# A latent-trunk kernel: the fourth expert's transposed hidden rows in a buffer of their own, transposes two weight units up

## The chip, the core and the metric

The kernel runs on one core of one Trainium2 chip. The metric is the device time of one execution in microseconds (us). A core has five engines with queues of their own: TensorE (PE in the profile; its weight loads are PEld), VectorE (DVE), ScalarE (ACT), GpSimd (POOL) and SyncE (SP, which here issues the loads of the weights). They meet only at semaphores.

## What is computed

A two-layer trunk over 256 tokens of width 1024 (float32). Each layer has a mixer (attention and a short convolution in the first, a convolution module in the second) and then a mixture of experts: 16 experts in 4 groups of 4; a router picks for every token one group and two experts in it. Cut to what matters here:

```python
def moe_ffn(h, router_w, router_b, w1, w3, w2):
    t = h.reshape(-1, shape[-1])
    gates = route(t, router_w, router_b)
    out = jnp.zeros_like(t)
    for e in range(N_EXPERTS):
        y = (jax.nn.silu(t @ w1[e]) * (t @ w3[e])) @ w2[e]
        out = out + gates[:, e:e + 1] * y
```

w1[e] and w3[e] are 1024 x 512, w2[e] is 512 x 1024.

## The kernel before

**Precision.** Every product is made of three matmuls: an operand is rounded (`whi`, `xghi`, `hidThi`), the remainder is kept beside it (`wlo`, `xglo`, `hidTlo`), and `three` (L1822 to L1829) adds high by high, low by high and high by low. ScalarE does the roundings, VectorE the remainders.

**Turns and units.** A layer's experts run in four *turns*, one for a group of four experts and up to 128 gathered rows. In layer 0 all four turns are alike (three in a hardware loop, the fourth written out behind it, since it fetches no rows for a next turn). In layer 1 three are alike (two in the loop, the third behind it with `prepare`, in which the rows for a last turn are gathered with 32 matmuls, `gather`), and the last is the *wide* turn (`wide`), where each expert has its own rows. A turn runs through 48 *weight units* of 512 KB, j = 0 to 47, in the order of `expert_order`, four units for each matrix:

```
units  0-3 w1 e0    4-7 w3 e0    8-11 w1 e1   12-15 w3 e1  16-19 w2 e0  20-23 w1 e2
units 24-27 w3 e2  28-31 w2 e1  32-35 w1 e3   36-39 w3 e3  40-43 w2 e2  44-47 w2 e3
```

For every unit SyncE loads `raw` (8 slots, L550), ScalarE rounds it to `whi` (6 slots, `round_turn`, L796), VectorE subtracts to `wlo` (6 slots, `rest_turn`, L1463), and TensorE runs two times three matmuls of 512 columns (L1827 to L1829). ScalarE may round unit j once TensorE is through with unit j - 6 (it waits for `w_used` of j - 5 units); a `raw` slot is free for its next load when VectorE has subtracted the unit in it.

**Hidden rows.** After expert e's w1 and w3, ScalarE makes `silu` and VectorE `hid` (`hid_mul`, L1528, placed ahead of the subtraction of unit W13[e] + 13, which is 45 for the fourth expert). TensorE transposes `hid` in four pieces into bank BT of PSUM (`transpose_hidden`, L2205), ScalarE rounds it to `hidThi` (`hidT_round`, L966), VectorE makes `hidTlo` (`hidT_remainder`, L1533), and the expert's first w2 unit waits for that (`hidT_rest`). There is one pair `hidThi`, `hidTlo` for all experts.

**Where these steps stand** was set by one table, HID_T = [12, 20, 32, 44]: TensorE transposes ahead of unit HID_T[e]; ScalarE and VectorE do their step ahead of unit HID_T[e] + 6, and for the fourth expert, whose 50 lies beyond the turn, behind unit 47. In the looped turns TensorE also transposes the next turn's gathered rows (`xrow`, L2154, eight pieces, `rows_turned(0)`) right behind the fourth expert's hidden transposes, in the `prepare` turn it runs `gather` there (L2128), and both signal `gathered`. On that signal GpSimd fetches further rows, and ScalarE and VectorE round them (`xg_round`, L982 and L1491) after unit 1 of the next turn; ahead of the wide turn `xg_round` comes before the rounding of that turn's unit 0.

In the wide turn the previous turn's result is scattered at units 10, 13, 16 and 19 (`scatter`, L2198, which waits for VectorE's `x_add`, L1511), and the wide experts' own results are scattered from unit 46 on.

Of the kernel before, what the change touches and what calls it, by code (L numbers as in the profile page):

```python
# [12 lines left out]
P = 128  # L13
# [215 lines left out]
def program(nc, x, c, ctx, c_ctx, norm1_g, norm2_g, w_mod, b_mod, na_w_in, na_rpb, sc_conv_w, ab_w_out,  # L229
            cf_pw1_w, cf_pw1_b, cf_dw_w, cf_dw_b, cf_ln_g, cf_ln_b, cf_pw2_w, cf_pw2_b, router_w, router_b,  # L230
            moe_w1, moe_w3, moe_w2, final_g, consts, bias_scratch, mod_scratch, tok_scratch0, tok_scratch1, y_scratch0, y_scratch1, out):
    with ExitStack() as stack:
# [76 lines left out]
        hid = at("hid", [P, FF], 28)  # L309
        hidThi = at("hidThi", [P, FC, P], 30, F32R)  # L310
        hidTlo = at("hidTlo", [P, FC, P], 32, F32R)
        yg = at("yg", [P, D], 34)
        yhi = at("yhi", [P, D], 38, F32R)
        ylo = at("ylo", [P, D], 42, F32R)
# [175 lines left out]
        def mod_filled(eng, v):  # L490

            eng.wait_ge(mod_in[v % 4], 16 * ((v + 2) // 4))

        def moe_slot(tile, n):
            return tile[:, n % (RAW if tile is raw else SPL), :]
# [287 lines left out]
        def _(eng):  # L783
# [162 lines left out]
            def experts(L):  # L946
# [16 lines left out]

                def hidT_round(tn, e):
                    tn.wait(eng, "hid_T", e + 1)
                    A.copy(hidThi[:], ps[:, BT, :].rearrange("p (k n) -> p k n", k=4)).then_inc(tn.sem("hidT_rounded"), 1)  # L966

                def y_round(tn):
                    tn.wait(eng, "y_scaled", 1)
# [18 lines left out]
                def turn(tn, first=HEAD, ahead=HEAD):  # L988

                    for j in range(first, W_GROUP):  # L990
                        for e in range(PER_GROUP):
                            if j == W13[e] + 4 + 5:
                                silu_of(tn, e)
                            if j == HID_T[e] + 6:
                                hidT_round(tn, e)
                        round_turn(tn, j)
                    hidT_round(tn, PER_GROUP - 1)
                    for j in range(W_GROUP, W_GROUP + ahead):
                        round_turn(tn, j)
                    if ahead:  # L1000
                        xg_round(tn.g, 1)
# [17 lines left out]
                def wide(i):  # L1019
                    tn = wide_turn(i)  # L1020
                    if i:
                        gate_copy(tn)
                        wide_xg_round(tn, i, 0)
                    for j in range(W_GROUP):
                        for a in range(2):
                            if j == WIDE_SPREAD[a] + 7:
                                spread_copy(tn, a)
                        if j == 8 and i == 0:
                            y_round(Turn(L, GROUPS - 1, sems))
                        for e in range(PER_GROUP):  # L1030
                            if j == W13[e] + 4 + 5:
                                silu_of(tn, e)
                            if j == HID_T[e] + 6:
                                hidT_round(tn, e)
                            if e and j == WIDE_GATHER[e] + 4 + e // 2 * 2:
                                wide_xg_round(tn, i, e)
                            if j == WIDE_Y[e] + 8:
                                wide_y_round(tn, e)
                        round_turn(tn, j)
                    hidT_round(tn, PER_GROUP - 1)  # L1040
                    for e in range(2, PER_GROUP):
                        wide_y_round(tn, e)

# [101 lines left out]
        def _(eng):  # L1145
# [207 lines left out]
            def experts(L):  # L1353
# [176 lines left out]

                def hidT_remainder(tn, e):
                    tn.wait(eng, "hidT_rounded", e + 1)
                    V.tensor_tensor(hidTlo[:], ps[:, BT, :].rearrange("p (k n) -> p k n", k=4), hidThi[:], ALU.subtract) \  # L1533
                     .then_inc(tn.sem("hidT_rest"), 1)

                def wide_select():
# [23 lines left out]
                def turn(tn, first=HEAD, ahead=HEAD, prepare=False):  # L1560

                    looped = tn.spill is None
                    for j in range(first, W_GROUP):
                        if prepare and j == 10:
                            wide_select()
                        if prepare and j == WIDE_PREFIX + 8:
                            wide_places()
                        if looped:
                            if j == 5:
                                y_scale(tn)  # L1570
                        for e in range(PER_GROUP):
                            if j == W13[e] + 8 + 5:
                                hid_mul(tn, e)
                            if j == HID_T[e] + 6:
                                hidT_remainder(tn, e)
                        if looped and not ahead and j == BACK:
                            at_ = tn.g + C_SLOT
                            link(set_spread(cst[:, at_:at_ + 1]))
                            eng.wait_ge(y_back, 16 * (L + 1))
                            for t in range(NT):  # L1580
                                link(V.tensor_tensor(xres[:, t, :], xres[:, t, :], yback[:, t, :], ALU.add))
                        rest_turn(tn, j)
                    hidT_remainder(tn, PER_GROUP - 1)
                    for j in range(W_GROUP, W_GROUP + ahead):
                        rest_turn(tn, j)
                    if ahead:
                        xg_remainder(tn.g, 1)
# [31 lines left out]
                def wide(i):  # L1619
# [12 lines left out]
                    for j in range(W_GROUP):  # L1632
# [7 lines left out]
                        for e in range(PER_GROUP):  # L1640
                            if j == W13[e] + 8 + 5:
                                if e == 0:
                                    tn.wait(eng, "spread_set", 1)
                                hid_mul(tn, e)
                            if j == HID_T[e] + 6:
                                hidT_remainder(tn, e)
                            if e and j == WIDE_GATHER[e] + 4 + e // 2 * 2:
                                wide_xg_rest(tn, i, e)
                            if j == WIDE_Y[e] + 5:
                                wide_y_scale(tn, e)  # L1650
                            if j == WIDE_Y[e] + 9:
                                wide_y_rest(tn, e)
# [2 lines left out]
                                if j == SCATTER[k] + 6:  # L1655
                                    x_add(last, k)
                        rest_turn(tn, j)
                    hidT_remainder(tn, PER_GROUP - 1)
                    for e in range(2, PER_GROUP):
                        wide_y_scale(tn, e)  # L1660
                        wide_y_rest(tn, e)
# [159 lines left out]
        def _(eng):  # L1821
# [275 lines left out]
            def experts(L):  # L2097
# [112 lines left out]
                def turn(tn, prepare=False, ahead=True):  # L2210
                    looped = tn.spill is None
                    for j in range(W_GROUP):
# [19 lines left out]
                        if name == "w2":  # L2232
                            if q == 0:
                                tn.wait(eng, "hidT_rest", e + 1)
                            for half in range(2):
                                cut = slice(half * HALF, (half + 1) * HALF)
                                ins = three(ps[:, BY + half, :], hidThi[:, q, :], hidTlo[:, q, :],
                                            moe_slot(whi, n)[:, cut], moe_slot(wlo, n)[:, cut],
                                            e == 0 and q == 0, e == PER_GROUP - 1 and q == 3)
                        else:  # L2240
# [36 lines left out]
                def wide(i):  # L2277
# [8 lines left out]
                    for j in range(W_GROUP):  # L2286
# [27 lines left out]
                        if name == "w2":  # L2314
# [3 lines left out]
                                    tn.wait(eng, "y_scaled", min(e, 2))  # L2318
                            for half in range(2):
                                cut = slice(half * HALF, (half + 1) * HALF)  # L2320
                                ins = three(ps[:, WIDE_BY[e] + half, :], hidThi[:, q, :], hidTlo[:, q, :],
                                            moe_slot(whi, n)[:, cut], moe_slot(wlo, n)[:, cut], q == 0, q == 3)
                        else:
                            if name == "w1" and q == 0 and (e or i):
# [137 lines left out]

W13 = [expert_order().index((e, "w1")) * 4 for e in range(PER_GROUP)]

HID_T = [12, 20, 32, 44]
SCATTER = [10, 13, 16, 19]

XG_AT = 2
# [96 lines left out]
```

## Time and profile before

| | us |
|---|---|
| median of 3 runs (lowest, highest) | 1009.28 (1009.09, 1009.70) |
| the profiled execution | 1009.37 |
| its span, first to last instruction | 1007.6 |

So 1.8 us of the profiled execution lie around its span, and it stands 0.09 us over the median. The mean granted TensorE clock over the span is 0.986 of full speed.

A row of the timeline is: start in us from the span's start, duration, engine, line, operation, output<-inputs, shapes, count; in brackets the idle time of that engine ahead of it, and what ended it. Matmuls are pipelined and their ends are modelled: the next one starts before the end that is written, so a stream is best read from start to start. "issue" is idle time for which the profile shows no releaser.

### The profile page before, as it was taken

The page shows a single profiled execution, that of the slowest core. Times are in us where ns is not written, and L with a number is a line of the kernel's source. Part 1 is how long each engine was busy: PE and PEld are TensorE (multiplying, and loading weights), DVE is VectorE, ACT ScalarE, POOL GpSimd, SP SyncE. Part 2 cuts the span into 40 slices and gives each one's busy share as a digit, 9 for nine tenths or more (in the row PEclk, how much of TensorE's full clock was granted, in tenths as well). Part 3 has the DMA queues.
Part 4 walks back from the last instruction along what each step waited for, and adds up shares of the span by engine and source line. Part 5 has one row for each costly group of instructions (what it writes and reads, how often), then busy time and mean ns, then how long its engine had stood idle before and what let it go on. Part 6 is the DMA issues. An engine that isn't in the chain of part 4 may idle for free.

```text
span 1007.6 us, 16757 instructions
## 1 busy us (share of the span) xinstructions
PE 954.8 (95%) x6004; PEld 758.9 (75%) x6004; DVE 754.3 (75%) x929; ACT 620.5 (62%) x769; POOL 113.6 (11%) x181
## 2 busy tenths in 40 slices
PE   5899999999999999999978999898999999999995
PEld 3688885788887878878857885677787878888784
DVE  1544378558998989989966634666998989888994
ACT  3824326435878778777844424426888877758772
POOL 3290000103001000000000632010001000000000
PEclk9999999999999999999998999999999999999999
DMA  9997859669999999999969765929999999988971
GB/s 364 354 259 260 285 197 336 208 259 298 395 396 360 392 370 359 395 338 382 392 229 307 206 214 160 368 83 369 396 396 360 393 376 344 392 330 277 353 272 44
DMA packets 145810, 314.07 MB, mean 312 GB/s; under 512 B 12904, under 2 KB 43920, under 8 KB 145736
## 3 DMA queue, kind: packets, MB, share of 16 engines
q1 hardware_dynamic: 135360, 286.53, 79.5%
q0 software_dynamic: 10048, 26.45, 7.8%
q8 instruction: 45, 0.74, 0.3%
q14 instruction: 29, 0.24, 0.1%
q10 hardware_dynamic: 328, 0.11, 0.0%
HBM read 298.64 MB, written 9.75 MB: 306 GB/s over the span
## 4 chain that ended last, share of the span: by engine, by line
PE 79%; DVE 8%; DMA 7%; issue 2%; ACT 2%; SPq 0%; DVEq 0%; ACTq 0%
PE ps L1827 17%; PE ps L1829 16%; PE ps L1828 16%; DMA raw<-in_w_mod 3%; PE ps L2390 3%; DMA raw<-in_moe_w 3%; PE ps L1839 2%; DVE wlo L1463 2%; PE ps L1929 2%; PE ps L1931 2%; PE ps L1930 2%; PE ps L2416 2%; PE ps L2417 2%; PE ps L2418 2%; PE ps L1947 1%
## 5 line engine op out<-in xcount | busy, mean ns | idle before, releaser
L1463 DVE TENSOR_TENSOR wlo<-raw,whi 128x1024 fp32r<-128x1024 f32 x384 | 454.4, 1220 | 40.7 <-ACT whi L796 37.6
L796 ACT CAST whi<-raw 128x1024 fp32r<-128x1024 f32 x384 | 398.5, 1052 | 109.9 <-PE ps L1829 75.3
L1827 PE MATMUL ps<-whi,xghi 128*128 128x512 f32 x480 | 193.7, 404 | 3.7 <-DVE wlo L1463 2.6
L1829 PE MATMUL ps<-wlo,xghi 128*128 128x512 f32 x480 | 190.6, 397 | 0.0
L1828 PE MATMUL ps<-whi,xglo 128*128 128x512 f32 x480 | 190.6, 397 | 0.0
L1827 PEld LDWEIGHTS ps<-whi,xghi 128*128 128x128 f32 x480 | 91.0, 190 | 26.8 <-DVE wlo L1463 6.0
L1827 PE MATMUL ps<-whi,hidThi 128*128 128x512 f32 x256 | 102.6, 401 | 6.6 <-DVE hidTlo L1533 5.2
L1829 PEld LDWEIGHTS ps<-wlo,xghi 128*128 128x128 f32 x480 | 91.1, 190 | 21.6
L1828 PEld LDWEIGHTS ps<-whi,xglo 128*128 128x128 f32 x480 | 91.3, 190 | 20.2
L1158 DVE TENSOR_TENSOR wlo<-raw,whi 128x1024 fp32r<-128x1024 f32 x56 | 73.0, 1338 | 40.5 <-ACT whi L791 40.3
L1829 PE MATMUL ps<-wlo,hidThi 128*128 128x512 f32 x256 | 101.8, 398 | 0.0
L1828 PE MATMUL ps<-whi,hidTlo 128*128 128x512 f32 x256 | 101.6, 397 | 0.0
L791 ACT CAST whi<-raw 128x1024 fp32r<-128x1024 f32 x56 | 56.8, 1046 | 44.3 <-DMA raw<-in_na_w_in 18.5
L1839 PE MATMUL ps<-raw,pair 128*32 128x256 f32 x768 | 58.7, 413 | 10.6 <-DMA raw<-in_w_mod 7.6
L1827 PEld LDWEIGHTS ps<-whi,hidThi 128*128 128x128 f32 x256 | 48.6, 190 | 19.5 <-issue 7.5
L1829 PEld LDWEIGHTS ps<-wlo,hidThi 128*128 128x128 f32 x256 | 48.5, 189 | 11.5
L1828 PEld LDWEIGHTS ps<-whi,hidTlo 128*128 128x128 f32 x256 | 48.6, 190 | 11.1
L1839 PEld LDWEIGHTS ps<-raw,pair 128*32 128x32 f32 x768 | 20.5, 115 | 32.6 <-issue 14.9
L1929 PE MATMUL ps<-hThi,whi 128*128 128x256 f32 (+1 forms) x144 | 44.2, 307 | 0.1
L1931 PE MATMUL ps<-hTlo,whi 128*128 128x256 f32 (+1 forms) x144 | 42.3, 294 | 0.0
L1930 PE MATMUL ps<-hThi,wlo 128*128 128x256 f32 (+1 forms) x144 | 42.3, 294 | 0.0
L2416 PE MATMUL ps<-fThi,whi 128*128 128x256 f32 x128 | 37.3, 292 | 3.2 <-DVE fTlo L1748 3.2
(354 smaller groups left out, 1455.6 us busy)
## 6 DMA issues: line engine op xcount, KB each, us to landing
raw<-in_moe_w SPq DMA_DIRECT2D x384, 512.0 KB, 6.7
raw<-in_w_mod SPq DMA_DIRECT2D x96, 512.0 KB, 6.9
raw<-in_na_w_in SPq DMA_DIRECT2D x24, 512.0 KB, 8.9
raw<-in_cf_pw_w SPq DMA_DIRECT2D x24, 512.0 KB, 8.6
mods<-mod_scratch POOLq DMA_DIRECT2D x9, 512.0 KB, 6.5
raw<-in_ab_w_out SPq DMA_DIRECT2D x8, 512.0 KB, 5.9
urep<-uT SPq DMA_DIRECT2D x64, 35.5 KB, 2.9
urep<-uT POOLq DMA_DIRECT2D x64, 35.5 KB, 2.5
```

The lines of the kernel that those rows point to most:

```text
L791: A.copy(whi[:, n % SPL, :], raw[:, u % RAW, :]).then_inc(w_rounded, 1)
L796: A.copy(whi[:, (MOE_W[tn.L] + j) % SPL, :], raw[:, (MOE_U[tn.L] + j) % RAW, :]).then_inc(tn.sem("w_rounded"), 1)
L1158: V.tensor_tensor(wlo[:, n % SPL, :], raw[:, u % RAW, :], whi[:, n % SPL, :], ALU.subtract).then_inc(unit_done, 1)
L1463: V.tensor_tensor(wlo[:, n % SPL, :], raw[:, (MOE_U[L] + j) % RAW, :], whi[:, n % SPL, :], ALU.subtract).then_inc(tn.sem("unit_done"), 1)
L1827: T.matmul(dst, lhi, rhi, start=first, stop=False)
L1828: T.matmul(dst, llo, rhi, start=False, stop=False)
L1829: return T.matmul(dst, lhi, rlo, start=False, stop=last)
L1839: ins = T.matmul(ps[q * QUAD:(q + 1) * QUAD, bank, 0:QW], pair[:, k, :], raw[:, u % RAW, q * QW:(q + 1) * QW], start=(k == 0), stop=(k == ...
L1929: T.matmul(dst, wpart(n0, k, 0, m * P, P), acts(k, 0), start=(k == 0), stop=False)
L1930: i2 = T.matmul(dst, wpart(n0, k, 1, m * P, P), acts(k, 0), start=False, stop=False)
L1931: i3 = T.matmul(dst, wpart(n0, k, 0, m * P, P), acts(k, 1), start=False, stop=(k == KC - 1))
L2416: T.matmul(dst, wpart2(done_n, k, 0, m * P, P), a0, start=(k == 0), stop=False)
```

## The change

- HID_T[3] goes from 44 to 42, so the fourth expert's transposes, and with them the rows' transposes or the `gather`, stand ahead of unit 42, in the middle of the third expert's w2.
- A table HID_ROUND = [18, 26, 38, 47] takes the place of HID_T[e] + 6. For the first three experts the values are the same. The fourth expert's rounding and remainder stand ahead of unit 47 now, not behind it.
- Since units 42 and 43 still read the third expert's `hidThi` and `hidTlo`, the fourth expert gets its own pair: `lastThi`, `lastTlo` in looped turns, `wideThi`, `wideTlo` in the wide turn. `hidden_T` picks the pair.

```diff
+        last_hidT = (at("lastThi", [P, FC, P], 46, F32R), at("lastTlo", [P, FC, P], 48, F32R))
+        wide_hidT = (at("wideThi", [P, FC, P], 68, F32R), at("wideTlo", [P, FC, P], 70, F32R))
...
+        def hidden_T(tn, e):
+
+            return (hidThi, hidTlo) if e < PER_GROUP - 1 else wide_hidT if tn.after else last_hidT
...
-                    A.copy(hidThi[:], ps[:, BT, :].rearrange("p (k n) -> p k n", k=4)).then_inc(tn.sem("hidT_rounded"), 1)
+                    A.copy(hidden_T(tn, e)[0][:], ps[:, BT, :].rearrange("p (k n) -> p k n", k=4)).then_inc(tn.sem("hidT_rounded"), 1)
...
-                            if j == HID_T[e] + 6:
+                            if j == HID_ROUND[e]:
                                 hidT_round(tn, e)
                         round_turn(tn, j)
-                    hidT_round(tn, PER_GROUP - 1)
...
-                            if j == HID_T[e] + 6:
+                            if j == HID_ROUND[e]:
                                 hidT_remainder(tn, e)
...
-                    hidT_remainder(tn, PER_GROUP - 1)
...
-                                ins = three(ps[:, BY + half, :], hidThi[:, q, :], hidTlo[:, q, :],
+                                ins = three(ps[:, BY + half, :], hidden_T(tn, e)[0][:, q, :], hidden_T(tn, e)[1][:, q, :],
...
-HID_T = [12, 20, 32, 44]
+HID_T = [12, 20, 32, 42]
+HID_ROUND = [18, 26, 38, 47]
```

**TensorE, looped turn of layer 0**, before: the last matmuls of unit 43, the transposes of `hid` and of the rows, and unit 44.

```order
L1828 MATMUL ps<-whi,hidTlo 128x512
L1829 MATMUL ps<-wlo,hidThi 128x512
L207 REGISTER_ALU
L2205 MATMUL ps<-cst,hid 128x128 [waits hid_set]
L2205 MATMUL ps<-cst,hid 128x128 x3
L2229 ISA
L2154 MATMUL ps<-cst,xrow 128x128 [waits rows_of]
L2154 MATMUL ps<-cst,xrow 128x128 x7
L207 REGISTER_ALU
L1827 MATMUL ps<-whi,hidThi 128x512 [waits hidT_rest,unit_done]
```

The same in the changed kernel (its lines are three higher); what follows is unit 42.

```order
L1831 MATMUL ps<-whi,hidTlo 128x512
L1832 MATMUL ps<-wlo,hidThi 128x512
L207 REGISTER_ALU
L2208 MATMUL ps<-cst,hid 128x128 [waits hid_set]
L2208 MATMUL ps<-cst,hid 128x128 x3
L2232 ISA
L2157 MATMUL ps<-cst,xrow 128x128 [waits rows_of]
L2157 MATMUL ps<-cst,xrow 128x128 x7
L207 REGISTER_ALU
L1830 MATMUL ps<-whi,hidThi 128x512 [waits unit_done]
```

Unit 44, two units on, carries the wait for `hidT_rest` and reads `lastThi`. **VectorE, layer 0's last turn**, before:

```order
L1528 SCALAR_TENSOR_TENSOR hid<-silu,gturn,ps 128x512 [waits w_used,silu_set]
L1463 TENSOR_TENSOR wlo<-raw,whi 128x1024 [waits w_rounded] x3
L1533 TENSOR_TENSOR hidTlo<-ps,hidThi 128x512 [waits hidT_rounded]
L1483 TENSOR_TENSOR yg<-ps,g2keep 128x512 [waits y_put,w_used]
L1483 TENSOR_TENSOR yg<-ps,g2keep 128x512
```

and in the changed kernel:

```order
L1532 SCALAR_TENSOR_TENSOR hid<-silu,gturn,ps 128x512 [waits w_used,silu_set]
L1467 TENSOR_TENSOR wlo<-raw,whi 128x1024 [waits w_rounded] x2
L1538 TENSOR_TENSOR lastTlo<-ps,lastThi 128x512 [waits hidT_rounded]
L1467 TENSOR_TENSOR wlo<-raw,whi 128x1024 [waits w_rounded]
L1487 TENSOR_TENSOR yg<-ps,g2keep 128x512 [waits y_put,w_used]
```

The remainder of the fourth expert's hidden rows moved ahead of the subtraction of unit 47; `hid` itself stays where it was, ahead of unit 45's. **ScalarE, end of the wide turn**, before:

```order
L796 CAST whi<-raw 128x1024 [waits w_used,raw_in5]
L796 CAST whi<-raw 128x1024 [waits w_used,raw_in6]
L796 CAST whi<-raw 128x1024 [waits w_used,raw_in7]
L966 CAST hidThi<-ps 128x512 [waits hid_T]
L1012 CAST yhi_107<-yg 128x1024 [waits y_scaled]
```

and in the changed kernel:

```order
L802 CAST whi<-raw 128x1024 [waits w_used,raw_in5]
L802 CAST whi<-raw 128x1024 [waits w_used,raw_in6]
L972 CAST wideThi<-ps 128x512 [waits hid_T]
L802 CAST whi<-raw 128x1024 [waits w_used,raw_in7]
L1017 CAST yhi_111<-yg 128x1024 [waits y_scaled]
```

The rounding of the hidden rows moved ahead of that of unit 47; no engine's count of these instructions changed.

## Rows read from the trace of the kernel before

**Rows 1.** Page, sections 1 and 4: busy by engine, chain by engine
```profile
PE 954.8 (95%) x6004; PEld 758.9 (75%) x6004; DVE 754.3 (75%) x929; ACT 620.5 (62%) x769; POOL 113.6 (11%) x181
...
PE 79%; DVE 8%; DMA 7%; issue 2%; ACT 2%; SPq 0%; DVEq 0%; ACTq 0%
```

**Rows 2.** Tile view, who waited for hidTlo: us in total, times
```profile
  PE ps L1827: 5.2, 7
```

**Rows 3.** Timeline (start, duration in us), end of layer 0's first turn
```profile
299.38 0.40 PE L1827 MATMUL ps<-whi,hidThi 128*128 128x512 f32 x1
...
302.19 0.60 PE L2205 MATMUL ps<-cst,hid 128*128 128x128 f32 x4
...
302.62 1.04 PE L2154 MATMUL ps<-cst,xrow 128*128 128x128 f32 x8
...
302.82 0.59 ACT L966 CAST hidThi<-ps 128x512 fp32r<-128x512 f32 x1 [2.19 <-PE ps L2205]
...
303.44 0.69 DVE L1533 TENSOR_TENSOR hidTlo<-ps,hidThi 128x512 fp32r<-128x512 f32 x1 [1.55 <-ACT hidThi L966]
...
304.28 0.47 PE L1827 MATMUL ps<-whi,hidThi 128*128 128x512 f32 x1 [0.62 <-DVE hidTlo L1533]
```

**Rows 4.** Timeline, four transposes whose result nobody waits for
```profile
256.12 0.60 PE L2205 MATMUL ps<-cst,hid 128*128 128x128 f32 x4
...
256.48 0.48 PE L1827 MATMUL ps<-whi,xghi 128*128 128x512 f32 x1
```

**Rows 5.** Timeline, TensorE, end of layer 0's last turn
```profile
513.73 0.60 PE L2205 MATMUL ps<-cst,hid 128*128 128x128 f32 x4
...
515.82 0.47 PE L1827 MATMUL ps<-whi,hidThi 128*128 128x512 f32 x1 [1.49 <-DVE hidTlo L1533]
```

**Rows 6.** Timeline, TensorE, end of the wide turn
```profile
983.02 0.60 PE L2205 MATMUL ps<-cst,hid 128*128 128x128 f32 x4
...
985.06 0.47 PE L1827 MATMUL ps<-whi,hidThi 128*128 128x512 f32 x1 [1.45 <-issue]
```

**Rows 7.** Timeline, TensorE, end of layer 1's last looped turn
```profile
904.36 3.74 PE L2128 MATMUL ps<-pick,htok 128*128 128x128 f32 x32
...
907.86 0.48 PE L1827 MATMUL ps<-whi,hidThi 128*128 128x512 f32 x1
```

**Rows 8.** Timeline, start of the wide turn, three engines
```profile
908.14 1.07 ACT L982 CAST xghi<-ps 128x512 fp32r<-128x512 f32 x2 [2.99 <-PE ps L2128]
...
910.20 2.36 DVE L1463 TENSOR_TENSOR wlo<-raw,whi 128x1024 fp32r<-128x1024 f32 x2 [3.99 <-ACT whi L796]
...
913.81 0.50 PE L1827 MATMUL ps<-whi,xghi 128*128 128x512 f32 x1
...
920.60 1.08 ACT L1006 CAST xg2hi<-ps 128x512 fp32r<-128x512 f32 x2 [1.21 <-PE ps L2154]
...
940.22 0.50 PE L2198 MATMUL ps<-yhi,spread 128*128 128x512 f32 x1 [0.68 <-DVE xres L1511]
```

**Rows 9.** Timeline, VectorE and ScalarE beside units 40 to 43, three turns
```profile
297.60 0.74 DVE L1528 SCALAR_TENSOR_TENSOR hid<-silu,gturn,ps 128x512 f32<-128x512 f32 x1
...
298.26 3.63 DVE L1463 TENSOR_TENSOR wlo<-raw,whi 128x1024 fp32r<-128x1024 f32 x3
...
299.58 1.05 ACT L796 CAST whi<-raw 128x1024 fp32r<-128x1024 f32 x1 [0.35 <-PE ps L1829]
...
509.93 0.74 DVE L1528 SCALAR_TENSOR_TENSOR hid<-silu,gturn,ps 128x512 f32<-128x512 f32 x1
...
979.05 0.73 DVE L1528 SCALAR_TENSOR_TENSOR hid<-silu,gate_of,ps 128x512 f32<-128x512 f32 x1
```

**Rows 10.** SyncE's waits (us, times, longest); issues: KB, us to landing
```profile
SPq L550 <- DVE wlo L1463: 377.9, 368, 14.5
...
raw<-in_moe_w SPq DMA_DIRECT2D x384, 512.0 KB, 6.7
```

**Rows 11.** One stretch: busy PE, PEld, DVE, ACT, POOL; PEclk, DMA, GB/s
```profile
896.70:900.30 3.60, 3.60 (x11) 2.82 (x11) 2.63 (x3) 0.94 (x1) 0.00 (x0) 0.56 1.01 377
```

More of the change, by code:

```diff
@@ L1039, in wide @@
                         round_turn(tn, j)
-                    hidT_round(tn, PER_GROUP - 1)
                     for e in range(2, PER_GROUP):
@@ L1532, in hidT_remainder @@
                     tn.wait(eng, "hidT_rounded", e + 1)
-                    V.tensor_tensor(hidTlo[:], ps[:, BT, :].rearrange("p (k n) -> p k n", k=4), hidThi[:], ALU.subtract) \
+                    hi, lo = hidden_T(tn, e)
+                    V.tensor_tensor(lo[:], ps[:, BT, :].rearrange("p (k n) -> p k n", k=4), hi[:], ALU.subtract) \
                      .then_inc(tn.sem("hidT_rest"), 1)
@@ L1573, in turn @@
                                 hid_mul(tn, e)
-                            if j == HID_T[e] + 6:
+                            if j == HID_ROUND[e]:
                                 hidT_remainder(tn, e)
@@ L1644, in wide @@
                                 hid_mul(tn, e)
-                            if j == HID_T[e] + 6:
+                            if j == HID_ROUND[e]:
                                 hidT_remainder(tn, e)
@@ L1657, in wide @@
                         rest_turn(tn, j)
-                    hidT_remainder(tn, PER_GROUP - 1)
                     for e in range(2, PER_GROUP):
@@ L2320, in wide @@
                                 cut = slice(half * HALF, (half + 1) * HALF)
-                                ins = three(ps[:, WIDE_BY[e] + half, :], hidThi[:, q, :], hidTlo[:, q, :],
+                                ins = three(ps[:, WIDE_BY[e] + half, :], hidden_T(tn, e)[0][:, q, :], hidden_T(tn, e)[1][:, q, :],
                                             moe_slot(whi, n)[:, cut], moe_slot(wlo, n)[:, cut], q == 0, q == 3)
```

## The prediction

> **What bounds the kernel now.** I read the page first. TensorE is busy for 95% of the span and holds 79% of the chain that ended last; VectorE and the DMA hold 8% and 7% [rows 1]. "Busy" alone proves little here, since the ends of matmuls are modelled, so I went to the timeline of a looped turn and read from start to start. Unit 42 starts at 299.38 and the transposes behind unit 43 at 302.19 [rows 3]: 12 matmuls in 2.81 us, 0.234 us each, 1.40 us a unit. 288 such matmuls are 67.4 us; the turns of layer 0 follow each other in 70.5 us (the hidden transposes stand at 302.19 in the first turn and at 513.73 in the fourth, three turns on [rows 3, 5]). So in a turn TensorE streams, and only what interrupts the stream counts. The next view is who waits for the tile `hidTlo`: TensorE, 7 times, 5.2 us [rows 2]. The timeline shows the place: behind unit 43 the transposes run, then ScalarE rounds, VectorE subtracts, and only then does unit 44 start [rows 3]. Nothing else of that turn's end is exposed.
>
> **The stall, by turn.** What the stall costs is not the idle time in the brackets, since it is counted from modelled ends, but the distance of the starts less what the transposes cost when nobody waits for them. Four of those take 0.36 us from their start to the next unit's [rows 4]; the gather's 32 matmuls, of the same shape, go in 3.50 us, 0.11 each [rows 7], so eight rows' transposes are 0.87.
> - Looped turn with rows' transposes: 304.28 - 302.19 - 0.36 - 0.87 = 0.86 us [rows 3]. There are five: turns 1 to 3 of layer 0 and 1 and 2 of layer 1, all with the same 0.62 us in the bracket (5 x 0.62 + 1.49 for the next case leave 0.6 of the 5.2 us for the seventh wait, the first expert's in layer 1's first turn, which the change doesn't touch). 5 x 0.86 = 4.3 us.
> - Last turn of layer 0, without rows: 515.82 - 513.73 - 0.36 = 1.73 us [rows 5].
> - Wide turn: 985.06 - 983.02 - 0.36 = 1.68 us [rows 6]. The view calls it "issue", but the order of the work is the same.
> - `prepare` turn: none, the gather covers it; unit 44 starts right behind it [rows 7].
>
> The sum is 7.7 us. By the brackets alone it would be 5 x 0.62 + 1.49 + 1.45 = 6.0 us [rows 3, 5, 6]; I take the distances and keep 6.0 as the low end.
>
> **Does the change remove it all?** The transposes move, they don't multiply: four of `hid`, eight of the rows or the gather, at the same cost, ahead of unit 42. What has to be ready there is `hid`. In the steady turn VectorE finishes it at 298.34, unit 42 starts at 299.38 [rows 3, 9]: 1.0 us to spare. In layer 0's last turn `hid` is finished at 510.67 and unit 42 stands two units ahead of 513.73, at 510.92: 0.25 us. In the wide turn it is 979.78 against 980.21: 0.43 us [rows 5, 6, 9]. From VectorE's end to TensorE's start 0.15 us pass (303.44 + 0.69 to 304.28 [rows 3]), so both just hold, with 0.10 us left in the tighter one.
>
> Then the new pair has to be ready at unit 44. ScalarE starts its rounding 0.63 us after the transposes start and takes 0.59 [rows 3]. VectorE has the subtractions of units 45 and 46 ahead of the remainder, 1.21 us each (3.63 for three [rows 9]). Steady turn: VectorE is free at 298.26 + 2.42 = 300.68, ScalarE is ready at 299.38 + 0.63 + 0.59 = 300.60, the remainder is there at about 301.4, unit 44 would start at 299.38 + 1.23 + 2.81 = 303.42. Last turn of layer 0: 510.67 + 2.42 + 0.69 + 0.15 = 513.9 against 510.92 + 0.36 + 2.81 = 514.1. Wide turn: 979.78 + 3.26 = 983.0 against 983.4. So nothing of the stall should be left, though the last two are covered by 0.2 and 0.4 us only. If that cover is gone, the excess comes back us for us.
>
> What stands behind the moved steps in the queues: on ScalarE the rounding of unit 47, which would have started at 299.58 [rows 9], waits for the transposes and the new rounding and ends near 301.7; VectorE's subtraction of unit 47 ends near 302.9, where before it ended at 301.89 (298.26 + 3.63). Unit 47 itself is due on TensorE at 303.42 + 3 x 1.40 = 307.6. The SyncE load into that slot is issued 1.0 us later; it lands 6.7 us after issue [rows 10], at 309.6, and TensorE is through with unit 1 of the next turn, on which its rounding (unit 7's) waits anyway, near 303.42 + 6 x 1.40 = 311.8. That hides it. The first roundings of the next turn had been held up behind the old rounding and are no longer. The move to other buffers costs nothing: same shapes, same engines.
>
> **The start of the wide turn.** The moved gather has a second effect. Before, ScalarE waits 2.99 us for it and VectorE then stands idle for 3.99 us, until 910.20 [rows 8], and from there VectorE is late twice: the wide turn's first unit starts at 913.81, where 907.86 + 4 x 1.40 + 0.08 = 913.54 would do (0.27 us), and the scatter at 940.22 shows 0.68 us in the bracket, which is 0.85 from start to start, since a modelled end lies 0.17 behind the pace. With the gather two units up it ends at 905.05; ScalarE can round unit 0 when unit 42 is through, at 906.45, and VectorE starts at about 907.6, 2.6 us earlier. Not all of it lasts. At 920.60 ScalarE waits 1.21 us for TensorE's own transposes of the second expert's rows [rows 8], and they come at most 0.27 us earlier; there VectorE's lead shrinks to some 0.6 us. I take 0.55 us for the whole, with 0.27 as the low end (the first wait alone) and 1.12 as the high one (both).
>
> **Sum.** 7.7 + 0.55 = 8.25 us off the profiled execution's 1009.37: 1001.1; off the median, 0.09 lower, 1001.0. From the low ends (6.0 + 0.27) to the high ones (7.7 + 1.12) it is 1003.0 to 1000.5. Layer 0's share should come through to the end: in the code the loads of the second mixer's first matrices wait for slots that TensorE itself frees behind the last turn.
>
> **Rivals.**
> 1. *The thin covers don't hold.* In layer 0's last turn and in the wide turn either `hid` comes late to unit 42 or the remainder late to unit 44. For it: 0.10 to 0.4 us of slack. Against it: the sums above are made of measured durations. If half of 1.73 + 1.68 stays, the time is 1001.0 + 1.7 = 1002.7; if all of it stays, 1004.4.
> 2. *The clock.* Between 896.7 and 900.3 the granted clock is 0.56 [rows 11], half speed in the main (1.2 of 2.4 GHz), behind a run of one-column products in the `prepare` turn. It costs (1 - 0.56) x 3.6 = 1.6 us. The change shifts everything behind it by some us, so such a stretch may grow, shrink or fall away: 1001.0 plus or minus 1.6. Against it: the stretch begins 4 us ahead of the place that changes in that turn. The Trainium skill (TensorE: Matmul & The Clock Gate, "What's actually happening") says that the window by which the clock is set runs on its own and does not start with the kernel. By that rule, one such stretch appearing or vanishing would give 1002.6 or 999.4; the trace shows the stretches but not what sets where they end.
> 3. *The loads become the bound (slower).* The place is the slot of unit 47, refilled 1.0 us later in each of the eight turns while TensorE wants its successor 0.9 us earlier. By the sum above the load lands 2.2 us before it is needed. From a landing later by more than that, each further us is paid in every turn. From 1.0 us over it the gain is gone (8 x 1.0 against 8.25); at 1.3 us over it the time is 1009.3 + 10.4 - 8.25 = 1011.5. For it: SyncE waits 368 times for VectorE's subtractions [rows 10], so a late subtraction does hold up loads. Against it: the 2.2 us, and that the first roundings of each next turn are freed.
> 4. *The stall only changes its place:* unit 42 waits as long for `hid` as unit 44 did for the remainder. Within 0.2% of before. Only `hid` 2 us later than in [rows 9] would do that.
>
> **How the numbers follow.** Forecast 0.68, thin covers 0.12, clock 0.14 (half to each side), loads 0.03, stall in a new place 0.03. The range takes the bounds of the sum, most of the thin covers and either clock case: 999.4 to 1003.8. A measurement of this kernel can tell about 0.2%, 2 us, from no change. Faster by over that: the first three, 0.94; within it 0.03; slower 0.03.
>
> **What would show it.** TensorE's waits for the tiles `lastTlo` and `wideTlo` absent from the views (the one wait for `hidTlo` left is the first expert's in layer 1's first turn); transposes of `hid` two units behind unit 41's end with 0.36 us to the next start; the period of layer 0's turns 0.9 us shorter, 69.6; VectorE starting the wide turn's unit 0 some 2.6 us earlier against TensorE, and no more than half of the wait at the scatter left. The forecast is wrong if TensorE's rows show idle time ahead of the transposes (rival 1 or 4), if ScalarE's roundings of units 5 to 8 of a turn wait for the DMA (rival 3), or if stretches with a clock under 1 lie elsewhere or last longer (rival 2).

## The result, and the profile after

| | before | changed |
|---|---|---|
| median (lowest, highest) | 1009.49 (1009.09, 1010.46), 4 runs | 1001.10 (999.59, 1002.17), 4 runs |
| the profiled execution | 1009.37 | 999.59 |
| its span | 1007.6 | 997.8 |
| mean granted clock | 0.986 | 0.985 |

The ratio of the changed kernel to the one before is 0.9896, with a 95% interval of 0.9868 to 0.9923. It is faster by more than the 0.2% that the prediction named. The median lies at the forecast, 1001.0; but the ratio, taken on 1009.28, gives 998.8 (996.0 to 1001.5), just under the range of the prediction, which ended at 999.4, and the profiled execution lost 9.8 us where 8.25 were forecast. The ratio is not the quotient of the two medians: that is 0.9917, 8.4 us. Why the two differ, the eight times do not show.

The page of the changed kernel, the same two lines as in [rows 1]:

```profile
PE 954.2 (96%) x6004; PEld 757.9 (76%) x6004; DVE 751.0 (75%) x929; ACT 620.7 (62%) x769; POOL 114.8 (12%) x181
...
PE 79%; DMA 9%; DVE 7%; ACT 2%; issue 2%; SPq 1%; DVEq 0%; ACTq 0%
```

The shares hardly move, since the stall was never more than 1% of the span. The view of the tile `lastTlo` says what became of it. Its lines are the instructions that write it, the idle time ahead of them, and who waited for it:

```profile
L1538 DVE TENSOR_TENSOR lastTlo<-ps,lastThi x7: 683/692/692, 302.7 to 895.0; 128x512 fp32r<-128x512 f32 x7
its engine sat idle before it (us, times) until:
who waited for it (us, times):
```

There is nothing under "who waited", and nothing under the idle times. Before, TensorE waited 7 times for the remainder [rows 2]; the one wait of the changed kernel, 0.2 us for `hidTlo`, is the first expert's in layer 1's first turn. The end of a looped turn, to be read against [rows 3] (timeline of TensorE; start, duration):

```profile
301.41 0.60 PE L2208 MATMUL ps<-cst,hid 128*128 128x128 f32 x4
...
301.84 1.04 PE L2157 MATMUL ps<-cst,xrow 128*128 128x128 f32 x8
...
302.64 0.47 PE L1830 MATMUL ps<-whi,hidThi 128*128 128x512 f32 x1
```

This is unit 42's start now, not unit 44's: 302.64 - 301.41 = 1.23 us for all twelve transposes, the 0.36 + 0.87 of the prediction. In layer 0's last turn (against [rows 5]), VectorE's `hid`, TensorE's transposes and unit 42, VectorE's remainder, and the step from unit 43 to unit 44:

```profile
509.83 0.74 DVE L1532 SCALAR_TENSOR_TENSOR hid<-silu,gturn,ps 128x512 f32<-128x512 f32 x1
...
510.82 0.60 PE L2208 MATMUL ps<-cst,hid 128*128 128x128 f32 x4
...
511.18 0.48 PE L1830 MATMUL ps<-whi,hidThi 128*128 128x512 f32 x1
...
512.76 0.68 DVE L1538 TENSOR_TENSOR lastTlo<-ps,lastThi 128x512 fp32r<-128x512 f32 x1
...
513.83 0.40 PE L1832 MATMUL ps<-wlo,hidThi 128*128 128x512 f32 x1
...
514.06 0.39 PE L1830 MATMUL ps<-whi,lastThi 128*128 128x512 f32 x1
```

`hid` ends at 510.57, the transposes start at 510.82; the remainder ends at 513.44, unit 44 starts at 514.06 and only 0.23 us behind its predecessor: no wait. The two margins are 0.25 and 0.6 us. In the wide turn (against [rows 6]) it is the same, 0.23 us from unit 43 to unit 44:

```profile
975.26 0.39 PE L1832 MATMUL ps<-wlo,hidThi 128*128 128x512 f32 x1
...
975.49 0.40 PE L1830 MATMUL ps<-whi,wideThi 128*128 128x512 f32 x1
```

The start of the wide turn, to be read against [rows 7, 8]:

```profile
894.19 3.74 PE L2131 MATMUL ps<-pick,htok 128*128 128x128 f32 x32
...
897.68 0.48 PE L1830 MATMUL ps<-whi,hidThi 128*128 128x512 f32 x1
...
897.96 1.07 ACT L988 CAST xghi<-ps 128x512 fp32r<-128x512 f32 x2 [2.04 <-PE ps L2131]
...
900.49 1.23 DVE L1467 TENSOR_TENSOR wlo<-raw,whi 128x1024 fp32r<-128x1024 f32 x1 [2.98 <-ACT whi L802]
...
906.13 0.39 PE L1830 MATMUL ps<-whi,xghi 128*128 128x512 f32 x1
...
912.77 0.59 ACT L1011 CAST xg2hi<-ps 128x512 fp32r<-128x512 f32 x1 [1.59 <-PE ps L2157]
...
932.24 0.50 PE L2201 MATMUL ps<-yhi,spread 128*128 128x512 f32 x1 [0.52 <-DVE xres L1515]
```

The gather ends two units earlier; ScalarE rounds its result at 897.96 at once, VectorE stands idle for 2.98 us in place of 3.99 and begins the wide turn's subtractions at 900.49, 5.6 us ahead of TensorE's first unit of that turn (906.13). Before, it was 3.6 us ahead (913.81 - 910.20), so the lead grew by 2.0 us where the prediction had 2.6. At 912.77 ScalarE waits 1.59 us for the second expert's rows, and the wait at the scatter is 0.52 us in place of 0.68.

**Where the 9.8 us are.** The spans, cut at the same instructions in five profiles (two of the kernel before, three of the changed one; e1, e2 and e12 are runs of the study below). All times are from start to start.

| stretch | before | e2, before | changed | e1, changed | e12, changed |
|---|---|---|---|---|---|
| start to layer 0's first unit | 237.76 | 237.75 | 238.70 | 241.85 | 237.55 |
| to its first hidden transposes | 18.36 | 18.38 | 19.44 | 18.99 | 18.36 |
| **to the scatter of its last turn** | 267.68 | 267.79 | 263.82 | 263.84 | 264.15 |
| second mixer, to layer 1's first unit | 164.38 | 166.08 | 162.55 | 167.07 | 163.45 |
| to its first hidden transposes | 22.11 | 20.66 | 21.99 | 22.07 | 22.47 |
| **two turns on** | 141.81 | 141.87 | 139.77 | 139.72 | 139.51 |
| **to the wide turn's first hidden transposes** | 79.93 | 79.89 | 77.93 | 79.47 | 79.49 |
| **to the last scatter** | 66.36 | 66.40 | 64.53 | 64.56 | 64.48 |
| to the end | 9.21 | 9.08 | 9.07 | 9.03 | 9.04 |

The bold rows hold what the change touches. They lose 9.7 us between the two first profiles, but 8.2 to 8.4 us between the two profiles of the kernel before and e1 or e12. The difference is in the main one thing, a stretch at half speed in the `prepare` turn. The other rows differ by up to 4.5 us among profiles in which their code is the same, and in the first two the time goes with the granted clock: from the start to layer 0's first unit it is 1.00 where the stretch takes 237.6 to 237.8 us, 0.99 at 238.7 and 0.97 at 241.9; from there to the first hidden transposes 0.91 at 18.4, 0.88 at 19.0 and 0.85 at 19.4. In the second mixer it runs from 0.93 to 0.97, the two shortest times at 0.97 and 0.95, the longest at 0.94.

### The profile page after: what moved, and what is told of

It is laid out like the page before. It is cut to its first block, busy times and chain, and to the rows that moved or that the text cites. A ratio compares the mean times of both kernels' runs of the same rounds, so it can differ in the third digit from the quotient of the medians.

```text
span 997.8 us, 16757 instructions
## 1 busy us (share of the span) xinstructions
PE 954.2 (96%) x6004; PEld 757.9 (76%) x6004; DVE 751.0 (75%) x929; ACT 620.7 (62%) x769; POOL 114.8 (12%) x181
## 4 chain that ended last, share of the span: by engine, by line
PE 79%; DMA 9%; DVE 7%; ACT 2%; issue 2%; SPq 1%; DVEq 0%; ACTq 0%
PE ps L1830 17%; PE ps L1832 17%; PE ps L1831 17%; DMA raw<-in_w_mod 3%; DMA raw<-in_na_w_in 3%; PE ps L2393 3%; PE ps L1842 2%; DMA raw<-in_moe_w 2%; PE ps L2419 2%; DVE wlo L1467 2%; PE ps L2420 2%; PE ps L2421 2%; PE ps L1932 1%; PE ps L2208 1%; PE ps L1933 1%
## 5 line engine op out<-in xcount | busy, mean ns | idle before, releaser
L1830 PE MATMUL ps<-whi,hidThi 128*128 128x512 f32 x192 | 76.8, 400 | 0.2 <-DVE hidTlo L1538 0.2
L1832 PE MATMUL ps<-wlo,hidThi 128*128 128x512 f32 x192 | 75.9, 395 | 0.0
L1831 PE MATMUL ps<-whi,hidTlo 128*128 128x512 f32 x192 | 75.7, 395 | 0.0
L1830 PEld LDWEIGHTS ps<-whi,hidThi 128*128 128x128 f32 x192 | 36.1, 188 | 8.7 <-issue 0.6
L1832 PEld LDWEIGHTS ps<-wlo,hidThi 128*128 128x128 f32 x192 | 36.1, 188 | 8.6
L1831 PEld LDWEIGHTS ps<-whi,hidTlo 128*128 128x128 f32 x192 | 36.1, 188 | 8.1
L711 POOL DMA_INDIRECT xrow<-tok_scratch,places x8 | 8.8, 1103 | 268.7 <-PE ps L2157 204.9
```

The lines of the kernel that those rows point to most:

```text
L1830: T.matmul(dst, lhi, rhi, start=first, stop=False)
L1831: T.matmul(dst, llo, rhi, start=False, stop=False)
L1832: return T.matmul(dst, lhi, rlo, start=False, stop=last)
```

## Experiments

Runs of one chip stand side by side: e1 to e4, e5 to e8, and e9 to e12. The kernel before had a median of 1013.43 (23 runs, 1007.62 to 1017.63), 1012.50 (19 runs, 1008.06 to 1016.83) and 1011.64 (11 runs, 1007.76 to 1015.69) there.

**e1, e2: both kernels once more, unaltered.**

> The changed kernel once more, unaltered, for its spread and its clock. Theory A (the change takes away TensorE's stall at the fourth expert's w2, 7.1 to 7.7 us, and 0.4 us at the start of the wide turn; what the first profile showed beyond that, 1.6 us of half-speed clock missing in the prepare turn and 1.8 us less in the second mixer, is chance): median 1001 to 1002, and in this profile a half-speed stretch may well stand in the prepare turn again. Theory B (the change itself also removes the half-speed stretch and shortens the second mixer): 999.5 in most runs, no stretch in the prepare turn, second mixer again 162.5 us from the first scatter to the first unit of layer 1.

> The kernel before, unaltered, for a second profile. Both theories: 1009 to 1010.5. Theory A: the half-speed stretches stand at other places or have other lengths than in the first profile. Theory B: the stretch of 3.6 us in the prepare turn is there again, and the second mixer again takes 164.4 us.

Measured: e1 1005.59 (6 runs, 999.65 to 1008.40), ratio 0.9914 (0.9885 to 0.9944); e2 1011.93 (10 runs, 1006.97 to 1017.97), ratio to the same code 0.9993 (0.9966 to 1.0021). The absolute medians miss the expectations, e1's by 3.6 us and e2's by 1.4 us; this chip's runs of the kernel before spread over 10 us, where the first four lay within 1.4. The ratio of e1, taken on 1009.28, gives 1000.6, inside the prediction's range. What the two theories say of the changed kernel came out for A. The busy times, clock, DMA share and GB/s of two stretches, the second mixer and the 3.6 us behind the one-column products of the `prepare` turn; first the changed kernel's first profile, then e1:

```profile
521.96:684.51 162.55, 151.32 (x1543) 116.77 (x1543) 91.50 (x154) 62.01 (x97) 39.29 (x77) 0.97 0.70 224
...
890.90:894.50 3.60, 3.60 (x21) 3.03 (x21) 3.41 (x4) 1.17 (x2) 0.00 (x0) 1.00 1.03 383
```

```profile
524.68:691.75 167.07, 153.87 (x1543) 118.88 (x1543) 91.62 (x154) 61.97 (x97) 39.15 (x77) 0.94 0.68 217
...
898.10:901.70 3.60, 3.60 (x11) 2.85 (x11) 2.67 (x3) 0.79 (x1) 0.00 (x0) 0.54 1.04 360
```

The last but two number is the granted clock. The stretch that was missing (1.00) is back in e1 (0.54), and the second mixer took 167.07 us at a clock of 0.94 in place of 162.55 at 0.97. The kernel before had 0.56 [rows 11] and, in its second mixer:

```profile
523.80:688.18 164.38, 151.46 (x1543) 117.94 (x1543) 91.75 (x154) 61.99 (x97) 39.18 (x77) 0.96 0.68 220
```

So these 1.6 and 1.8 us of the first profile are not of the change. Theory B falls. In e2 the half-speed stretch stood behind the one-column products again, with eight matmuls at half pace for seven (granted clock 0.60 from 897.1 to 900.7), which speaks for neither; but the second mixer took 166.08 us there, not the 164.4 of theory B.

**e3: the hidden transposes alone.** Edit on the changed kernel:

```diff
                             if j == HID_T[ee]:
                                 transpose_hidden(tn, ee)
-                                if looped and ee == PER_GROUP - 1 and ahead:
-                                    if prepare:
-                                        gather(tn.g + 1)
-                                    else:
-                                        eng.wait_ge(rows_of, ...)
-                                        rows_turned(0).then_inc(gathered, 1)
+                        if looped and ahead:
+                            if prepare and j == 44:
+                                gather(tn.g + 1)
+                            if not prepare and j == 44:
+                                eng.wait_ge(rows_of, ...)
+                                rows_turned(0).then_inc(gathered, 1)
```

> Only the fourth expert's hidden transposes move up to unit 42; the rows' transposes and the gather stay ahead of unit 44. Theory A: the stall is gone all the same, since the hidden rows are ready 0.9 us or more before unit 44; only the early start of VectorE in the wide turn is lost, 0.4 us: 1001.5. Rival (the gain comes with the rows and the gather): 1005 or more. VectorE would stand idle for about 4 us ahead of the wide turn again.

Measured: 1003.70 (6 runs), ratio 0.9911 (0.9886 to 0.9936), as e1's; the time is 2.2 us over the expected one, on the chip on which e1's was over it too. The periods of layer 0's turns are 69.53, 69.72 and 69.68 us, 0.1 us under the changed kernel's 69.80. The gather's share is seen at the wide turn, VectorE's start and TensorE's scatter:

```profile
905.77 2.36 DVE L1467 TENSOR_TENSOR wlo<-raw,whi 128x1024 fp32r<-128x1024 f32 x2 [5.28 <-ACT whi L802]
...
935.79 0.50 PE L2201 MATMUL ps<-yhi,spread 128*128 128x512 f32 x1 [0.68 <-DVE xres L1515]
```

VectorE is idle for 5.28 us, more than the 3.99 before the change, and the wait at the scatter is 0.68 us, as before the change; the turn from `prepare` to wide takes 79.86 us where e1 takes 79.47. So the stall goes with the hidden rows alone, and the gather is worth 0.4 us.

**e4: the transposes up, but one pair of buffers.** The fourth expert's rounding waits until unit 43 is through and stands behind unit 47's, the remainder too:

```diff
-            return (hidThi, hidTlo) if e < PER_GROUP - 1 else wide_hidT if tn.after else last_hidT
+            return (hidThi, hidTlo)
...
                     tn.wait(eng, "hid_T", e + 1)
+                    if e == PER_GROUP - 1:
+                        tn.wait(eng, "w_used", 44)
...
-HID_ROUND = [18, 26, 38, 47]
+HID_ROUND = [18, 26, 38, 99]
```

> Transposes two units up as in the change, but the fourth expert uses the common pair hidThi and hidTlo, so that ScalarE must wait until unit 43 is through, and rounds behind unit 47's rounding, as before. Theory A: each of the eight turns then waits at unit 44 for ScalarE (0.15 + 0.59), VectorE (0.03 + 0.69) and 0.15 back, with nothing as cover: 1.6 to 1.8 us each, 13 to 14 us over the changed kernel, 1014 to 1015, slower than before. Rival (the position of the transposes alone brings the gain and the buffer is incidental): 1001 to 1003.

Measured: 1016.48 (10 runs), ratio to the kernel before 1.0045 (1.0023 to 1.0068): slower, and by the ratios 13.2 us over e1. The end of layer 0's first turn, ScalarE, VectorE, TensorE:

```profile
308.24 0.59 ACT L974 CAST hidThi<-ps 128x512 fp32r<-128x512 f32 x1 [3.04 <-PE ps L1838]
...
308.85 0.69 DVE L1542 TENSOR_TENSOR hidTlo<-ps,hidThi 128x512 fp32r<-128x512 f32 x1 [2.40 <-ACT hidThi L974]
...
309.69 0.47 PE L1836 MATMUL ps<-whi,hidThi 128*128 128x512 f32 x1 [1.49 <-DVE hidTlo L1542]
```

1.49 us of idle time here; from start to start unit 44 comes 1.66 us later than the pace of 0.23 us, and so it is in every one of the eight turns (1.65 to 1.72), 13.3 us in all. Without the second pair the move does harm.

**e5, e6: one unit lower and one unit higher** (HID_T = [12, 20, 32, 43] and [12, 20, 32, 41]).

> The changed kernel with the fourth expert's transposes, rows and gather ahead of unit 43 instead of 42. From the start of the transposes it takes 0.63 + 0.59 + 0.03 + 0.69 + 0.15 = 2.1 us until the remainder is usable. A looped turn with rows gives 0.36 + 0.87 + 1.40 = 2.6 us of cover: no stall. Layer 0's last turn and the wide turn give 0.36 + 1.40 = 1.8 us: 0.3 us of stall each. Theory A: 0.6 to 0.8 us over the changed kernel. Rival (VectorE's queue, not the cover, sets it: it has unit 46's subtraction ahead): no more than 0.1 us of stall in the two.

> The changed kernel with the transposes ahead of unit 41. Theory A: now hid is late. It is finished 0.36 us (steady turn), 1.15 us (layer 0's last turn) and 0.97 us (wide turn) after unit 40 is through, plus 0.15 us to TensorE: stalls of 0.5 us in five turns, 1.3 and 1.1 us in the two, none in the prepare turn, 4.9 us in all, ahead of the transposes: 1006 beside a changed kernel of 1001. Rival (what VectorE has done by then moves up with TensorE, so hid comes in time): under 1 us.

Measured: e5 1006.47 (6 runs), ratio 0.9930 (0.9901 to 0.9959). In layer 0's last turn, the transposes and the last matmul of unit 43, VectorE's remainder, and unit 44:

```profile
516.01 0.60 PE L2208 MATMUL ps<-cst,hid 128*128 128x128 f32 x4
...
517.60 0.40 PE L1832 MATMUL ps<-wlo,hidThi 128*128 128x512 f32 x1
...
517.26 0.69 DVE L1538 TENSOR_TENSOR lastTlo<-ps,lastThi 128x512 fp32r<-128x512 f32 x1 [0.29 <-ACT lastThi L972]
...
518.10 0.47 PE L1830 MATMUL ps<-whi,lastThi 128*128 128x512 f32 x1
```

From 517.60 to 518.10 are 0.50 us, 0.27 over the pace, and in the wide turn 0.22 over it; no looped turn waits. That is theory A's 0.3 us (0.5 in the two turns together, too little for the times to tell), and VectorE waits for ScalarE there (0.29 us), not TensorE for VectorE's other work. e6 measured 1009.68 (10 runs), ratio 0.9965 (0.9944 to 0.9985). Its transposes in the first and the last turn of layer 0 and in the wide turn:

```profile
302.62 0.65 PE L2208 MATMUL ps<-cst,hid 128*128 128x128 f32 x4 [0.25 <-DVE hid L1532]
...
513.80 0.66 PE L2208 MATMUL ps<-cst,hid 128*128 128x128 f32 x4 [1.04 <-DVE hid L1532]
...
980.87 0.66 PE L2208 MATMUL ps<-cst,hid 128*128 128x128 f32 x4 [0.83 <-DVE hid L1532]
```

Now the idle time stands ahead of the transposes and the releaser is `hid`. From start to start it is 0.42 to 0.45 us in five turns, 1.20 and 0.99 us in the two others, 4.3 us in all against the 4.9 expected, and 5.1 us over e1 by the ratios. So of the three places 42 is the right one: at 41 `hid` is late, at 43 the remainder.

**e7: rows back at 44, gather at 42** (the edit of e3 with `prepare and j == 42`).

> The changed kernel with the rows' transposes of the looped turns back ahead of unit 44, but the gather of the prepare turn ahead of unit 42. Theory A: both gains together: periods of layer 0's turns 69.5 to 69.8 us, the wait at the scatter in the wide turn 0.69 us as in the changed kernel against 0.85 with the gather at unit 44. Time equal to the changed kernel's within 0.5 us. Rival (the gather's place is of no use): wait at the scatter 0.85 us and the prepare turn 0.4 us longer.

Measured: 1004.96 (6 runs), ratio 0.9919 (0.9890 to 0.9947). The periods are 69.67, 69.68, 69.68 us, the wait at the scatter 0.68 us from start to start, as e1's (0.85 before). As expected, within what the times can tell.

**e8 to e11: the one-column products cut in two.** In the `prepare` turn 28 one-column products stand ahead of unit 40. Edit:

```diff
-                        if prepare and j == WIDE_PREFIX + 12:
-                            wide_gates(0)
+                        if prepare and j in (WIDE_PREFIX + 12, WIDE_PREFIX + 13):
+                            wide_gates(0, (j - WIDE_PREFIX - 12,))
```

where part 0 runs the 16 for the gates and part 1 the 12 for the row numbers, with the signal. e8 and e11 are this on the changed kernel; e9 and e10 have e7's edit too.

> The changed kernel with the 28 one-column products of the prepare turn (3.0 us in one run ahead of unit 40) cut in two: 16 ahead of unit 40, 12 ahead of unit 41. Theory A with the clock as a rule of its own: the stretch of 2.6 to 3.6 us at half speed behind them, which stood in four of six profiles and costs about 1.6 us, does not appear; the prepare turn to wide turn period is 77.9 us as in the one profile of the changed kernel without a stretch. Rival (the stretch has to do with the time of the chip, not with these products): it stands there at half speed as often as before, period 79.5 us.

> The changed kernel with the two alterations joined: rows' transposes back ahead of unit 44 (gather stays at 42), and the one-column products cut in two. Expected from the traces: 5 x 0.12 us from the rows, about 1.2 us on average from the half-speed stretch that no longer stands in the prepare turn: 1.8 us under the changed kernel on the same chip. Rival (the stretch's absence in e8 was chance, as it was in two of nine profiles with the products in one run): the stretch is there in most of the next three profiles, and the gain is 0.6 us.

> The same kernel for one more profile. Products cut in two prevent the half-speed stretch: none in the prepare turn, from the first expert's transposes there to those of the wide turn 77.8 us. Rival: stretch of about 3 us, 79.4 us.

> The kernel of e8 for one more profile. Same expectation: no half-speed stretch in the prepare turn, 77.9 us. Rival: 79.5 us.

> The changed kernel for a third profile, beside the three with the products cut in two. By both theories the stretch stands here in about seven of ten cases (79.5 us), and the five looped turns and the fourth expert's step show no stall.

(The "four of six" of e8's expectation was a miscount: it was five of six.) The two parts in e8, and the 3.6 us behind the first:

```profile
892.70 1.84 PE L2175 MATMUL ps<-wsel,pick 128*128 128x1 f32 x16
...
895.88 1.39 PE L2182 MATMUL ps<-cst,pick 128*128 128x1 f32 x12
...
894.40:898.00 3.60, 3.60 (x24) 3.21 (x24) 3.60 (x4) 1.04 (x1) 0.00 (x0) 1.00 1.02 374
```

The granted clock stays at 1.00, and so it does over 892 to 899, behind both parts. With the products in one run, a stretch of 6 to 8 matmuls at half the pace followed in 8 of 10 profiles (not in the changed kernel's first and in e6); cut in two, in none of 4. From the `prepare` turn's first hidden transposes to the wide turn's the four take 77.92, 77.90, 77.91 and 77.93 us, and e12, in one run again, 79.49. By time: e8 1004.22, ratio 0.9910 (0.9880 to 0.9940); e9 1000.98 (6 runs), ratio 0.9892 (0.9862 to 0.9922); e10, e11 and e12, single executions, 1000.74, 1005.98 and 1000.39. e9 is the fastest kernel of the study by its ratio, but its interval overlaps those of e1 and e7 and the changed kernel's first (0.9896), and the one execution of the changed kernel on its chip, e12, was as fast: the 1.8 us expected for e9 cannot be read from the times. That it is better than the changed kernel rests on the trace, by 0.12 us in each of five turns and 1.6 us in the `prepare` turn.

e12 also misses its expectation in one place. In layer 0's last turn of this execution of the changed kernel TensorE does wait for `hid`. VectorE's `hid`, the end of unit 41 and the transposes:

```profile
508.08 0.74 DVE L1532 SCALAR_TENSOR_TENSOR hid<-silu,gturn,ps 128x512 f32<-128x512 f32 x1
...
508.40 0.40 PE L1832 MATMUL ps<-wlo,hidThi 128*128 128x512 f32 x1
...
508.87 0.66 PE L2208 MATMUL ps<-cst,hid 128*128 128x128 f32 x4
```

`hid` ends at 508.82, 0.05 us ahead of the transposes, and from 508.40 to 508.87 are 0.24 us over the pace. In the other eight profiles of this placement (hidden transposes at unit 42, a pair of their own) there is no such wait, though in e3 `hid` ends only 0.06 us ahead of the transposes, in the others 0.24 to 0.26. In the 60 us up to these transposes ScalarE waited for loads 21 times in e12, 7.6 us in all, and 7 to 11 times in the others, 2.4 to 3.9 us; that this is why VectorE came late is likely, but not shown.

## Why the prediction was right or wrong

**Right, and shown:** what bounds the kernel, the place of the stall, that it goes altogether (no wait for `lastTlo` or `wideTlo`), and that the gather helps the wide turn. The thin covers hold in the main. In layer 0's last turn `hid` has 0.25 us to spare, as worked out, and the remainder 0.6 us to unit 44, 0.5 with the handover of 0.15 taken off, where 0.2 was worked out; but in e12 the first of the two was used up, and 0.24 us of rival 1 came true. e4, e5 and e6 bear out the model behind it: the same five durations gave 1.6 to 1.8, 0.3, and 0.5, 1.3 and 1.1 us, and the runs showed 1.66, 0.27, and 0.42, 1.20 and 0.99. One of the five was too long where it was used for `hid`: where the transposes wait for VectorE's `hid` they start 0.05 or 0.06 us after its end (e12; e6: 302.62 after 302.56), not 0.15 us as the matmul behind the remainder does, and seven times 0.09 us is the 0.6 by which e6 came under its expectation.

Rival 3 did not come. Layer 1's first turn apart, where it was so before, no matmul of the looped turns waits for a weight unit; the units' loads land after 6.8 us (e12: 7.0) where it was 6.7, and ScalarE waits 29 to 37 us in all for them, where it was 34. Two of the signs named came short: the period of layer 0's turns is 69.8 us, not 69.6, and of the wait at the scatter 0.68 of 0.85 us are left, not half.

**Terms of the sum, against e1 and e12** (where the clock of the `prepare` turn is as before):
- Five looped turns: 0.86 us each were forecast, 0.73 us a turn in layer 0 came (70.53 to 69.80). The wait is gone in full; 0.1 us came back in the stream itself: in the second turn 280 intervals between matmuls that nothing interrupts took 65.32 us in place of 65.21. In e3 and e7, with the rows' transposes at unit 44, this 0.1 us is not paid. Why the stream is slower by 0.0004 us a matmul is open.
- Last turn of layer 0: 1.73 forecast; from its first hidden transposes to the scatter 56.18 us became 54.43 and in e1 54.42: 1.75. In e12, with the wait for `hid`, the row of the table is 0.3 us longer.
- Wide turn: 1.68 forecast, 1.84 measured on its row of the table, of which 0.16 is the scatter's shorter wait; that leaves the 1.68.
- Start of the wide turn: 0.55 forecast in all. On the rows of the table it is 0.43, with the 0.16 just named 0.6. The shares differ: the wait ahead of the wide turn's first unit was worth 0.4, not 0.27, and the scatter gave 0.16, not the 0.28 that the forecast amounts to. VectorE's lead shrank at the second expert's rows as described, but to 0.3 us behind them, not 0.6.
- Not foreseen: 0.6 us or more less in layer 1's first turn. The first w2 unit there waits 0.38 (e1: 0.33, e12: nothing) in place of 0.74 us, which is 0.4 to 0.7 of it. e2 shows 0.76, e5 nothing and e6 0.73, so part of it, perhaps all, is chance.

Together the stall and the wide turn's start gave 7.7 us of the 8.25. That part of the prediction was sized right to 0.6 us. That the touched rows lose 8.2 to 8.4 us all the same, and that the medians meet the forecast to 0.1 us, is luck: the unforeseen 0.6 us fill what the looped turns gave less.

**Wrong: the width of the range.** The result's ratio of 0.9896 is 2.2 us under the forecast, and outside the range by 0.6 us. The step that failed is in "How the numbers follow", with rival 2 behind it: for what the change does not touch the range allowed one half-speed stretch of 1.6 us coming or going, at one place, and put everything else there at nothing, without a reason. The table shows what moves with the same code: the second mixer 162.5 to 167.1 us, the way to layer 0's first unit 237.6 to 241.9, the stretch at layer 0's start 18.4 to 19.4. In the first profile three of them came together: the `prepare` stretch was missing (1.6 us), the second mixer was short (1.8 us), and the first two rows were long (2.0 us), net 1.4 us, which is nearly all by which its 9.8 us exceed the 8.2 to 8.4. On the chip of e1 to e4 single executions of the kernel before spread over 10 us, and go with the mean granted clock (0.973 to 0.986 in 23 runs, correlation with the time -0.76). The interval of the recorded ratio, 2.8 us to each side, laid about the forecast gives 998.2 to 1003.8, and that holds the result. Which stage gave the ratio its 0.6 us beyond the range is open, since there is one profile to four executions, and e1's repetition (1000.6) lies inside.

The rule of the Trainium skill (TensorE: Matmul & The Clock Gate, "What's actually happening") that the window runs on its own and not with the kernel fits what the profiles show: the same products, followed by the same matmuls, met a half-speed stretch in one execution of the changed kernel (e1) and not in another (its first profile). I had taken the clock as a rival, but let it act at one place only.

## What to carry to other kernels

A step that passes through two other engines and comes back costs its whole round trip when it stands directly ahead of its reader; count the round trip (here 2.1 us), put the step that much stream ahead, and give it a buffer of its own if the reader of the old contents is still at work. Check both sides of the move, the input that must be ready earlier and the output that must be ready in time: here one place of three fitted, and in one of three profiles of the changed kernel even that one was 0.24 us too early in one turn. For the range, take the spread of the stages that the change leaves alone from more than one profile.

## What the runs showed of the hardware

Two pieces of 16 and 12 one-column products with a weight unit between them left the clock at full speed in 4 of 4 profiles, the same 28 in one run of 3.0 us were followed by 2.6 to 3.6 us at half speed in 8 of 10, at 1.6 us where the same kernel is at hand without it (79.5 against 77.9 us from `prepare` to wide turn). And of a step that goes from TensorE over ScalarE and VectorE back to TensorE, more than the work was exposed: in e4, 0.59 and 0.69 us of work delayed the next unit by 1.66 us from start to start, so some 0.4 us (an estimate: 1.66 less 1.28) are the handovers between the engines.
